# Running sums of the decays in a chunked scan: 32 rows by one product, spread over the partitions by DMA, in place of 32 TensorE products

## What is computed

```
a_cs = jnp.cumsum(ac, axis=-1)                      # running sums of dt * a within a chunk
decay_in = jnp.exp(segsum(ac))                      # exp(a_cs[l] - a_cs[s]) for s <= l, else 0
cb = jnp.einsum('bclgn,bcsgn->bcgls', cc, bc)
y_diag = jnp.einsum('bcgls,bgrcls,bcsgrp->bclgrp', cb, decay_in, xc)
...
y_off = jnp.einsum('bclgn,bcgrpn,bgrcl->bclgrp', cc, prev_states, jnp.exp(a_cs))
```

## Time and profile before

| | |
|---|---|
| runs | 1393.98, 1396.18, 1398.44 us, median 1396.18 |
| profiled execution, its own time | 1395.54 us |
| its span in the trace | 1393.8 us |
| PE busy | 1342.9 us, 96% of the span |
| DVE busy | 370.7 us, 27% |
| ACT busy | 178.1 us, 13% |

### The profile page before, as it was taken

How to read it: one execution, slowest core, us unless ns; L and a number is a source line. 1 busy time by engine, 2 the same in 40 slices (tenths; PEclk the granted TensorE clock), 3 DMA queues, 4 the chain that set the end, 5 groups by cost and what they waited for, 6 DMA issues and landing times.

```text
span 1393.8 us, 18198 instructions
## 1 busy us (share of the span) xinstructions
PE 1342.9 (96%) x7707; PEld 860.1 (62%) x7707; DVE 370.7 (27%) x825; ACT 178.1 (13%) x376; POOL 62.0 (4%) x87
## 2 busy tenths in 40 slices
PE   6999998999999999989999999999999999999986
PEld 5888887888888888758755534434343443444432
DVE  3535885321111016933300010201111011011112
ACT  1231324010001001042100000000000100100002
POOL 2003310000000102000000000000000000000000
PEclk9999999999999999999999999999999999999998
DMA  8536722564546333410999999999999999999994
GB/s 265 205 124 237 263 91 91 182 202 128 176 149 211 99 121 121 128 43 16 352 402 402 402 397 398 392 402 394 405 399 393 403 392 404 387 377 404 390 404 196
DMA packets 169666, 381.48 MB, mean 274 GB/s; under 512 B 7660, under 2 KB 63516, under 8 KB 169530
## 3 DMA queue, kind: packets, MB, share of 16 engines
q1 hardware_dynamic: 161571, 358.96, 69.5%
q0 software_dynamic: 3184, 11.40, 2.7%
q10 hardware_dynamic: 4834, 9.99, 2.2%
HBM read 372.41 MB, written 9.01 MB: 274 GB/s over the span
## 4 chain that ended last, share of the span: by engine, by line
PE 88%; DVE 6%; DMA 3%; SPq 1%; issue 1%; ACT 1%; ACTq 0%; DVEq 0%
PE ps L1711 30%; PE ps L2176 16%; PE ps L2241 13%; PE ps L2191 8%; PE ps L2201 4%; DVE region L1415 3%; PE ps L1937 3%; PE ps L2252 2%; DMA big<-in_moe_w_down_dram 1%; PE ps L2133 1%; PE ps L2095 1%; PE ps L2144 1%; PE ps L2218 1%; DMA big<-in_w_in_even_dram 1%; PE ps L1720 1%
## 5 line engine op out<-in xcount | busy, mean ns | idle before, releaser
L1711 PE MATMUL ps<-big 128*128 128x264 f32 x1376 | 314.9, 391 | 3.4 <-DMA big<-in_w_in_even_dram 3.4
L1711 PEld LDWEIGHTS ps<-big 128*128 128x128 f32 x1376 | 264.3, 193 | 50.2 <-DMA big<-in_w_in_even_dram 3.5
L2176 PE MATMUL ps<-big,region 128*64 128x384 f32 (+3 forms) x1200 | 217.7, 459 | 6.5 <-DMA big<-in_moe_w_gate_dram 3.5
L2176 PEld LDWEIGHTS ps<-big,region 128*64 128x64 f32 (+1 forms) x1200 | 115.5, 147 | 104.3 <-issue 62.1
L1711 PE MATMUL ps<-region,big 128*128 128x264 f32 x704 | 160.0, 390 | 3.7 <-ACT region L965 3.7
L2241 PE MATMUL ps<-big,region 128*64 128x512 f32 (+1 forms) x608 | 157.6, 609 | 2.2 <-DMA big<-in_moe_w_down_dram 1.6
L1711 PEld LDWEIGHTS ps<-region,big 128*128 128x128 f32 x704 | 134.4, 192 | 27.3 <-issue 4.1
L2191 PE MATMUL ps<-big,region 128*64 128x384 f32 (+1 forms) x720 | 111.0, 460 | 0.0
L2241 PEld LDWEIGHTS ps<-big,region 128*64 128x64 f32 (+1 forms) x608 | 50.5, 146 | 95.0 <-issue 91.3
L2191 PEld LDWEIGHTS ps<-big,region 128*64 128x64 f32 x720 | 51.3, 137 | 56.6 <-issue 49.0
L1626 DVE TENSOR_TENSOR region<-region,ps 128x384 f32<-128x384 f32 (+1 forms) x24 | 12.1, 520 | 225.5 <-PE ps L2176 225.5
(11 more groups left out here) (371 smaller groups left out, 1032.0 us busy)
## 6 DMA issues: line engine op xcount, KB each, us to landing
big<-in_moe_w_up_dram SPq DMA_DIRECT2D x48, 1536.0 KB
big<-in_moe_w_gate_dram SPq DMA_DIRECT2D x40, 1536.0 KB
big<-in_moe_w_down_dram SPq DMA_DIRECT2D x40, 1536.0 KB
big<-in_w_in_even_dram SPq DMA_DIRECT2D x10, 2048.0 KB
big<-in_moe_w_gate_dram SPq DMA_DIRECT2D x16, 1024.0 KB
big<-in_moe_w_up_dram SPq DMA_DIRECT2D x16, 1024.0 KB
big<-in_moe_w_down_dram SPq DMA_DIRECT2D x16, 1024.0 KB
region<-in_moe_w_gate_dram SPq DMA_DIRECT2D x8, 1536.0 KB
```

The lines of the kernel that those rows point to most:

```text
L1711: ins = mm(ps[:, 0:T], w[:, c, cols:cols + P], src[:, c, :], start=c == 0, stop=c == nk - 1)
L2176: ins = mm(out, xg[:, 4 * j + c, 0:cap], w[:, c, r, :], start=j + c == 0, stop=j + c == 4)
```

## The change

Tile `cs` gets a third product: the 32 rows of running sums (16 heads, 2 chunks) as 32 partitions by 128 tokens. ScalarE copies it to SBUF (`cst`) and stores it in DRAM (`csd`, 16 KB). Once the store is complete and the region of the v rows is free, ScalarE's queue loads the rows back, eight rows (two groups of heads) at a time, each onto all 128 partitions, 512 KB a load: two loads ahead of the scan into the two halves of `CR`, and one more behind the exponentials of k = 1 and of k = 3. VectorE's L1300 and ScalarE's L888 read `CR` in place of a PSUM tile. The eight tiles `cr` are gone, with their 32 calls. Two semaphores get new names, which the loads share with earlier uses.

```
@@ psum_tiles
-    add("cs", ("cs_ready", 1))
+    add("cs", ("cs_ready", 1), ("dt_act", 4))
...
-            add(("cr", i), *((("seg_ready", 4 * i + 4),) + ((("ecs_ready", i - 3),) if i >= 4 else ())))
@@ build
+        csd = nc.dram_tensor("cs_rows", [32, P], F32).ap()
+        cst = big[32:64, 25600:25600 + P]
+        CR = [reg(8496 + 1024 * n, 1024).rearrange("p (k m) -> p k m", k=2) for n in range(2)]
@@ ScalarE, before the exponentials L861
+            act.wait_ge(sem("cs_ready"), 1)
+            a.activation(cst, tile("cs")[0:32, 64:192], ACT.Copy).then_inc(sem("dt_act"), 1)
+            act.wait_ge(sem("dt_act"), 4)
+            act.dma_start(csd, cst).then_inc(sem("x_loaded"), 16)
             act.wait_ge(sem("tot_ready"), 2)
@@ ScalarE, between the copies of vtok and of prevT
+            def broadcast_cs(j):
+
+                act.dma_start(CR[j % 2].rearrange("p k m -> p (k m)"),
+                              csd[8 * j:8 * j + 8, :].rearrange("(a h) l -> a (h l)", a=1).broadcast_to([P, 1024])).then_inc(
+                    sem(f"rows_in{j % 2}"), 16)
+
+            act.wait_ge(sem("x_loaded"), 80)
+            act.wait_ge(sem("gout_ready"), 1)
+            broadcast_cs(0)
+            broadcast_cs(1)
@@ ScalarE, in the scan
                 a.activation(dec[:, k % 2], dec[:, k % 2], ACT.Exp).then_inc(sem("dec_ready"), 1)
+                if k in (1, 3):
+                    broadcast_cs(2 + k // 2)
...
-                    a.activation(ecs[:, k % 2], tile(("cr", k))[:, :].rearrange("p (r l) -> p r l", r=4),
+                    act.wait_ge(sem(f"rows_in{k // 2 % 2}"), 48)
+                    a.activation(ecs[:, k % 2], CR[k // 2 % 2][:, k % 2].rearrange("p (r l) -> p r l", r=4),
@@ VectorE, in the scan
-                    filled(dve, ("cr", k))
+                    dve.wait_ge(sem(f"rows_in{k // 2 % 2}"), 16 * (k // 4 + 2))
...
-                        v.scalar_tensor_tensor(out=dec[:, k % 2, r], in0=tile(("cr", k))[:, P * r:P * (r + 1)],
+                        v.scalar_tensor_tensor(out=dec[:, k % 2, r], in0=CR[k // 2 % 2][:, k % 2, P * r:P * (r + 1)],
...
+                    filled(dve, ("cb", k))
                     dve.wait_ge(sem("dec_ready"), k + 1)
@@ TensorE, tile cs
-            done(mm(ps[:, 32:64], ones[:, :], adt[:, 0:32], start=True, stop=True))
+            mm(ps[:, 32:64], ones[:, :], adt[:, 0:32], start=True, stop=True)
+            done(mm(ps[0:32, 64:192], adt[:, 0:32], upper[:, :], start=True, stop=True))
@@ TensorE, in the scan
-                    ps = claim(("cr", k))
-                    for r in range(4):
-                        h = 16 * q + 4 * g + r
-                        ins = mm(ps[:, P * r:P * (r + 1)], adt[:, h:h + 1].broadcast_to([P, P]), upper[:, :],
-                                 start=True, stop=True)
-                    done(ins)
```

More of the change, by code:

```diff
@@ L488, in _ @@
             sp.dma_start(prow[0:120, 3, :], dw[128:248]).then_inc(sem("par_loaded"), 16)
-            sp.dma_start(wsn, i["gmlp_w_s"][0].rearrange("g i j -> i g j")).then_inc(sem("ws_loaded"), 16)
-            sp.dma_start(cbrows, i["state_ssd_conv"][0].rearrange("b k n -> (b k) n")).then_inc(sem("cb_loaded"), 16)
+            sp.dma_start(wsn, i["gmlp_w_s"][0].rearrange("g i j -> i g j")).then_inc(sem("rows_in0"), 16)
+            sp.dma_start(cbrows, i["state_ssd_conv"][0].rearrange("b k n -> (b k) n")).then_inc(sem("rows_in1"), 16)
             sp.dma_start(row16[0:1, 0:8], i["gmlp_w_s"][0, :, 0, 0:1].rearrange("g a -> a g"),
@@ L654, in _ @@
                    allow_small_or_imprecise_dtypes=True).then_inc(sem("const_ready"), 1)
-            pool.wait_ge(sem("ws_loaded"), 16)
+            pool.wait_ge(sem("rows_in0"), 16)
             g.affine_select(out=wsn, in_=wsn, compare_op=ALU.is_ge, fill=0.0, base=0,
@@ L734, in fetch_rows @@
                     out=xrow[0:cap, :], out_offset=None, in_=hrows[:, :],
-                    in_offset=bass.IndirectOffsetOnAxis(ap=rowidx[0:cap, 0:1], axis=0)).then_inc(sem("rows_loaded"), 16)
+                    in_offset=bass.IndirectOffsetOnAxis(ap=rowidx[0:cap, 0:1], axis=0)).then_inc(sem("rorows_in0"), 16)
             pool.wait_ge(sem("crw_stored"), 32)
@@ L1578, in rows_known @@
                 if s:
-                    dve.wait_ge(sem("rows_loaded"), t * 16 + 16 * s)
+                    dve.wait_ge(sem("rorows_in0"), t * 16 + 16 * s)
                 v.tensor_copy(rowidx[0:cap, :], psum[4][0:cap, BLK * P:BLK * P + 1]).then_inc(sem("rows_known"), 1)
@@ L1761, in _ @@
                 done(ins)
-            pe.wait_ge(sem("cb_loaded"), 16)
+            pe.wait_ge(sem("rows_in1"), 16)
             ps = claim("cbufT")
@@ L2088, in turn_rows_in @@
             def turn_rows_in(cap, value, n4, n5):
-                pe.wait_ge(sem("rows_loaded"), value)
+                pe.wait_ge(sem("rorows_in0"), value)
                 for half, n in enumerate((n4, n5)):
```

## The result

| | before | after |
|---|---|---|
| median, us | 1393.88 (20 runs, 1390.95 to 1399.10) | 1400.74 (20 runs, 1396.10 to 1406.19) |
| ratio after / before | | 1.0042, 95% interval 1.0031 to 1.0053 |
| profiled execution, us | 1395.54 (span 1393.8) | 1401.94 (span 1400.2) |
| TensorE busy, us | 1342.9 | 1338.1 |

The change made the kernel slower by 0.42%, about 5.9 us (0.0042 x 1394). The forecast was no change, with 1392.3 to 1399.5 us as its range: the measured 1400.74 us lies 1.2 us above the range, and the interval of the ratio leaves no change out. In the pages, TensorE has 4.8 us less to do and the span is 6.4 us longer.

The account below looks back on a forecast made before the run. VectorE's chain was taken to bound the scan from k = 1, hiding TensorE's work. Terms -2.3 + 0.6 = -1.7, plus 1.9 for the clock, gave +0.2 us: 1396.4 us against the 1396.18 median, range 1392.3 to 1399.5.

Parts of the forecast that it names:

- The removed cr: Start of the scan, k = 0 and 1: VectorE no longer waits for TensorE's cr tiles, gain 0.15 + 2.17 = 2.3 us.
- The third product, the copy and the store: Ahead of ScalarE's table load: added work delays mx and VectorE's chain by 0.6 us, bounds 0.3 to 0.9.
- The loads of rows: Row loads from DRAM before and during the scan: they land before they are needed, cost 0.
- rival 5: Rows land late and hold VectorE's in-order chain, giving the other sign, a slower kernel; chance 4%.
- Differences read from SBUF: VectorE's 32 differences in the scan: no change from the SBUF source, bounds 0.1 us below and 0 above.
- rival 4: VectorE's differences from SBUF are quicker by 65 ns each, shortening its chain by 2.1 us more; chance 5%.
- TensorE's clock: Behind a gap of about 5 us before the last y, TensorE's clock falls: +1.9 us, from 0 to 3.
- Rival 2: TensorE's clock holds through the gap before the last y, leaving -1.7 us; chance 31%.
- Nothing in the change touches its length: Mixture of experts, 680 to 1380 us: its length stays, so reaching its start early means ending early.

Follow-up runs that it names:

- e1: Changed kernel with GpSimd's multiplication of sample 7's state moved early, ahead of the scan; median 1396.04 us, ratio 1.0018.
- e6: Changed kernel with GpSimd's sample 7 multiplication moved early and 20 filler calls in TensorE's gap before the last y; median 1391.55 us, ratio 0.9978.
- e3: Changed kernel with the copy and store of the rows moved behind the two small exponentials; median 1401.17 us, ratio 1.0042.
- e12: Changed kernel with GpSimd's multiplication of sample 7 covering only half the columns, leaving computation out; one execution 1399.61 us.
- e2: Changed kernel with 20 filler matmul calls on TensorE just ahead of the wait for the last y; median 1394.12 us, ratio 0.9996.
- e9: Changed kernel with 20 tiny matmul calls at the start of TensorE's program, to shift its instruction transfers; 1398.11 us, ratio 1.0027.
- e5: Kernel before, unchanged, run again as a control; ratio 1.0000.
- e10: Kernel before with 29 tiny matmul calls at the start of TensorE's program, to shift its instruction transfers; 1398.63 us, ratio 1.0039.
- e11: e7 with 20 tiny matmul calls added at the start of TensorE's program; 1392.36 us, ratio 0.9976.
- e7: Changed kernel with GpSimd's sample 7 multiplication early, final state's matmuls ahead of the last y, its copies ahead of the Silu; median 1392.58 us, ratio 0.9979.
- e8: Kernel before with the same three moves as e7; median 1391.93 us, ratio 0.9975.

## Why the prediction was wrong

- *The removed cr, -2.3 us.* Right in the sum: the wait is gone, z 1 was in time, the last y of e1 starts 2.2 us earlier against mx, and e6 gives -1.6 in the stretch against a sum of -1.7. There is some luck in it. M waits 0.75 to 0.77 us for its inputs in place of 0.69 to 0.70, at each of the eight k, 0.5 us in all; the change puts a wait for cb of its own ahead of each M, which was not tried alone. The start of k = 0 and 1 gave 2.5 in place of 2.3, and 0.3 came from smaller places, among them the hold of 0.17 us of the kernel before.
- *The third product, the copy and the store, +0.6 us.* Right in size (+0.61). Its parts are not proved: e3 moved copy and store away and gained 0.2.
- *The loads of rows, 0.* Right; rival 5 (late rows) had no part, 4.1 us against the 8.1 taken as its bound.
- *"Differences read from SBUF", "I take no change"*, with "a slowing that no row shows, 0" as the bound above. **This is the step that failed.** 31 of 32 took the 0.34 us that they took before, so the comparison of the earlier trace rows was fair for an instruction alone, and rival 4 (quicker by 65 ns) fell too. But the row has no GpSimd instruction beside it. With both tensors in SBUF one difference stood until GpSimd's multiplication ended: +2.4 us. The trace of before did show such a slowing, in the rows at 126.51 and 132.04 us above (1.73 and 2.60 in place of 1.23 us), and GpSimd's multiplication in the scan. The Trainium skill says it ("SBUF — State Buffer", SBUF: two separate sides): a VectorE instruction with two SBUF inputs and a GpSimd instruction that reads SBUF exclude each other, the later one blocks for the whole instruction. e1 and e12 agree with it (352 ns at most without GpSimd beside it, 1.87 and 2.73 us with 1.06 and 1.93 us of it), but for which of the two is the later one: by the rows the held difference had begun at 190.5 us and GpSimd at 191.19, and GpSimd's starts are rough.
- *TensorE's clock, +1.9 us, behind a gap of "about 5 us".* Right mechanism and right gap (5.00 us); the size was 2.35 in the profile of after, by the stretch of e2 2.3. Every profile with such a gap shows the fall (after, e1, e3, e9, e12), at 1.4 to 2.4 us and 2.0 in the mean, measured from the last y to the rest of the output projection against before's 30.64 us, as the Trainium skill warns ("TensorE: Matmul & The Clock Gate", Why this matters for your kernels). Rival 2 (the clock holds, 31%) found no profile. What the term lacks is the other side: the gap of 3 us of the kernel before costs 1.6 us too, in two profiles of three (e5, e10), so the change adds less than the whole fall.
- *"Nothing in the change touches its length"*, of the stretch of the experts. Wrong: it shifts TensorE's program against its instruction transfers. The landing is 1.2 us longer, the clock fell behind the longer wait in all seven such profiles, and the means of the table differ by 2.5 us. e10 shows a price on a kernel that has nothing else of the change: +5.4 us, more than those 2.5. Its fall at 223 us is no part of it, as e5, whose ratio is 1.0000, has it too.

The sum for the two profiles: 0.2 forecast + 2.4 held + 0.45 clock = 3.1, as the stretch says (+3.1); with 0.8 ahead of the issue of the experts' weights, 2.1 behind it and 0.4 ahead of the first cs product that makes the 6.4 us of the spans. Whether it holds for the median is less sure. With the stretch's average of +1.8 and about 2.5 for the instruction transfers it comes to 4.3, against 5.9 measured. The last term is a difference of means over single profiles whose tails scatter by 2 to 4 us: e10 shows its direction, e9 and e11 don't confirm it in the time, and its size is good to about a us at best. Open are the 1.6 us that are left, why e11 is not quicker than e7, and why e7 is not quicker than e8 by the 2.4 us of its stretch.

One more step was loose, without effect: the range took 2.2 us of scatter below and 2.0 above; with 2.2 it would have ended at 1399.7 us, still short of 1400.74.

## What to carry to other kernels

Moving an operand of a VectorE instruction from PSUM to SBUF isn't free where it becomes the second source in SBUF and GpSimd computes at that time: list what GpSimd runs beside each such instruction, and move GpSimd's work to where VectorE reads PSUM or waits. Work taken from an engine that is hidden beneath another comes back as a gap, and a gap of TensorE costs clock; fill it with work that is due anyway (the final state with its copies: 90.43 to 85.48 us of the stretch, e1 to e7) and look who waits for that work next. A difference of up to 0.4% between two kernels (e10) can go with where the program's own instruction transfers fall, so compare a stretch of the trace before the whole time, over more than one profile of each kernel, and try the same kernel with its program shifted. Before a term is put at nothing because no row shows it, search the whole trace for such rows, by engine pairs and not by line alone.

## What the runs showed of the hardware

- A VectorE instruction that had begun (about 190.5 us) was held for an instruction of GpSimd whose row starts at 191.19 us; starts of GpSimd's rows are rough, the two ends (193.27 and 193.12) are what fits in both kernels. The held 128x128 instruction ended 0.15 us behind GpSimd's end (e12: 0.16), the held 128x1024 ones of the kernel before 1.09 us.
- A gap of 3.0 us of TensorE passed at the full clock in the profile of before and was followed by 3.4 us at half rate in those of e5 and e10; e5 is the same program.
- A single 16 KB instruction transfer inside a large weight load goes with a landing of 8.7 to 9.5 us in place of 8.0 to 8.1; how it delays the load was not tried.
